# GpSimd subtracts the first expert block's first five weight pieces, and the third block's up weights are requested half by half in another order

## The reference, cut to what matters

```python
def hierarchical_moe(h, w_router_group, w_router_expert, w1, w3, w2):
    xt = h.reshape(T, D); xf = xt.astype(jnp.float32)
    p_group = jax.nn.softmax(xf @ w_router_group, axis=-1)
    g_idx = jnp.argmax(p_group, axis=-1)
    g_w = jnp.take_along_axis(p_group, g_idx[:, None], axis=1)[:, 0]
    local = jnp.einsum('td,gde->tge', xf, w_router_expert)
    local = jnp.take_along_axis(local, g_idx[:, None, None], axis=1)[:, 0]
    top_logit, top_idx = lax.top_k(local, TOP_K)
    gate = jax.nn.softmax(top_logit, axis=-1) * g_w[:, None]
    flat_e = (g_idx[:, None] * EXPERTS_PER_GROUP + top_idx).reshape(-1)
    ...
    def run_block(args):
        xblk, e = args
        hid = jax.nn.silu(xblk @ w1[e]) * (xblk @ w3[e])
        return hid @ w2[e]
    yb = lax.map(run_block, (xb, block_e)).reshape(P, D)
    y = jnp.zeros((T + 1, D)).at[slot_tok].add(yb * slot_w[:, None])[:T]
```

## Time and profile before

| | |
|---|---|
| median of 3 runs | 1733.19 us (1732.63 to 1734.62) |
| profiled execution | 1734.33 us; its span is 1732.5 us |
| granted TensorE clock, mean | 0.979 |
| busy: PE, DVE, ACT, POOL | 1629.7, 1092.2, 861.4, 582.8 us |
| chain that ended last | PE 67%, DMA 15%, DVE 10%, issue 5% |
| DMA | 340.96 MB, mean 197 GB/s; in the experts' stage near 400 GB/s |

### The profile page before, as it was taken

One profiled execution on the slowest core, in us unless ns is written; L12 is line 12 of the kernel. 1 busy time (PEld: TensorE's weight loads), 2 busy tenths in 40 slices (PEclk: granted clock), 3 DMA queues, 4 the chain that ended last, 5 costly groups with the idle time before them and its releaser, 6 DMA issues.

```text
span 1732.5 us, 22014 instructions
## 1 busy us (share of the span) xinstructions
PE 1629.7 (94%) x7052; PEld 1206.6 (70%) x7052; DVE 1092.2 (63%) x1466; ACT 861.4 (50%) x1222; POOL 582.8 (34%) x354
## 2 busy tenths in 40 slices
PE   3899999999999999999999999895999999999996
PEld 3788888777878788778866887583655656656654
DVE  6776865371322458433575543236899999999996
ACT  4544533433222332234443234333878878877875
POOL 0578886333334335324302331110121222222221
PEclk9999999999999999999999999996999999999998
DMA  9343444133131163532211411356999999999993
GB/s 322 104 117 113 136 155 156 59 142 104 49 104 51 47 219 134 194 121 93 98 49 49 152 49 50 89 218 250 375 400 401 395 406 403 393 400 384 384 385 123
DMA packets 135423, 340.96 MB, mean 197 GB/s; under 512 B 14596, under 2 KB 66060, under 8 KB 110521
## 3 DMA queue, kind: packets, MB, share of 16 engines
q1 hardware_dynamic: 127938, 320.71, 49.9%
q0 software_dynamic: 5200, 8.41, 2.1%
q10 hardware_dynamic: 2215, 10.93, 1.6%
HBM read 329.78 MB, written 18.87 MB: 201 GB/s over the span
## 4 chain that ended last, share of the span: by engine, by line
PE 67%; DMA 15%; DVE 10%; issue 5%; ACT 2%; DVEq 0%; SPq 0%; POOLq 0%; ACTq 0%; POOL 0%
PE ps L767 17%; PE ps L769 17%; PE ps L768 17%; DMA ring<-in_w 13%; PE ps L739 6%; DVE parts L2335 3%; PE ps L981 2%; PE ps L749 2%; PE ps L1111 2%; DVE act_parts L2335 1%; DVE arena L2378 1%; PE ps L950 1%; PE ps L1009 1%; PE ps L1092 1%; DMA ring<-in_w_ada 1%
## 5 line engine op out<-in xcount | busy, mean ns | idle before, releaser
L2451 POOL TENSOR_TENSOR parts<-ring,parts 128x1024 fp32r<-128x1024 f32 x156 | 385.6, 2477 | 670.8 <-ACT parts L1209 571.9
L1209 ACT CAST parts<-ring 128x1024 fp32r<-128x1024 f32 x158 | 164.0, 1048 | 347.3 <-PE ps L769 312.1
L767 PE MATMUL ps<-parts,act_parts 128*128 128x512 f32 (+2 forms) x768 | 299.5, 390 | 4.2 <-DVEq L1864 3.0
L769 PE MATMUL ps<-parts,act_parts 128*128 128x512 f32 (+2 forms) x768 | 296.0, 385 | 0.0
L768 PE MATMUL ps<-parts,act_parts 128*128 128x512 f32 (+2 forms) x768 | 296.0, 385 | 0.0
L767 PE MATMUL ps<-act_parts,parts 128*128 128x512 f32 x640 | 252.0, 394 | 4.9 <-DVEq L1769 4.9
L768 PE MATMUL ps<-act_parts,parts 128*128 128x512 f32 x640 | 249.7, 390 | 0.0
L769 PE MATMUL ps<-act_parts,parts 128*128 128x512 f32 x640 | 249.6, 390 | 0.0
L1556 ACT CAST parts<-ring 128x1024 fp32r<-128x1024 f32 x144 | 144.4, 1047 | 83.7 <-PE ps L769 79.1
L767 PEld LDWEIGHTS ps<-parts,act_parts 128*128 128x128 f32 (+1 forms) x768 | 137.4, 179 | 64.8 <-issue 28.1
L2335 DVE TENSOR_TENSOR parts<-ring,parts 128x1024 fp32r<-128x1024 f32 x144 | 168.9, 1218 | 7.4 <-ACT parts L1556 7.2
(11 more groups left out here) (294 smaller groups left out, 2561.8 us busy)
## 6 DMA issues: line engine op xcount, KB each, us to landing
arena<-in_w SPq DMA_DIRECT2D x96, 1024.0 KB, 12.2
ring<-in_w SPq DMA_DIRECT2D x96, 1024.0 KB, 13.3
ring<-in_w_in SPq DMA_DIRECT2D x30, 1024.0 KB, 7.3
ring<-in_w_in SPq DMA_DIRECT2D x34, 512.0 KB, 5.1
ring<-in_w_ada SPq DMA_DIRECT2D x12, 1024.0 KB, 10.4
ring<-in_w_ret_out SPq DMA_DIRECT2D x8, 1024.0 KB, 6.3
ring<-in_w_out SPq DMA_DIRECT2D x8, 1024.0 KB, 7.4
ring<-in_w_in SPq DMA_DIRECT2D x16, 256.0 KB, 4.1
```

The source lines that it names most:

```text
L767: pe.matmul(o, lhs[1], rhs[0], start=start, stop=False)
L769: return pe.matmul(o, lhs[0], rhs[0], start=False, stop=stop)
L1209: act.copy(parts[:, g % 4, 0, :], ring[:, st.place(j), k * 1024:(k + 1) * 1024]).then_inc(dense_hi, 1)
L2451: pool.tensor_tensor(parts[:, g % 4, 1, :], ring[:, st.place(j), k * 1024:(k + 1) * 1024], parts[:, g % 4, 0, :].bitcast(F32), ALU.subtrac ...
```

## The change

Three edits. GpSimd subtracts pieces 2 to 6 of the first block, in a loop that stands behind its last dense piece and before it waits for the plan; DVE's subtractions of these five are gone, and it keeps piece 7. ACT casts piece 6 behind piece 5, before its two Exp. SP requests the third block's up weights in the order w1's second half, w3's first, w1's first, w3's second, with `planned(2)` read once; waits and places of each half are the same as before.

```diff
-            def expert_weights(j, expert, odd, landed=None, used=None):
+            def expert_weights(j, expert, odd, landed=None, used=None, halves=(0, 1)):
...
-                for n in range(2):
+                for n in halves:
...
-            up_weights(planned(2), 0, 32, 1)
+            third = planned(2)
+            for j, half in ((0, 1), (1, 0), (0, 0), (1, 1)):
+                expert_weights(j, third, 0, 32, 1, halves=(half,))
             up_weights(planned(3), 1, 48, 2)
-            expert_weights(2, planned(2), 0, 32, 1)
+            expert_weights(2, third, 0, 32, 1)
...
-            for n in range(2, 6):
+            for n in range(2, 7):
                 high(n, 0, 0)
...
             high_rows("moe0", 0)
-            high(6, 0, 0)
             high(7, 0, 0, used=(up_used, 1))
...
-            for n in (2, 3, 4, 5):
-                low(n, n - 2, 0)
-
             dve.wait_ge(gate_ready, 2)
...
             rest("moe0", 0, xgT)
-            for n in (6, 7):
-                low(n, n - 2, 0)
+            low(7, 5, 0)
...
             lows(len(PIECE_CHUNK))
 
+            for n in range(2, 7):
+                pool.wait_ge(piece_hi, n - 1)
+                pool.tensor_tensor(piece_parts(n)[:, 1, :], expert_place(n // 4, 0)[:, n % 4 * 1024:(n % 4 + 1) * 1024],
+                                   piece_parts(n)[:, 0, :].bitcast(F32), ALU.subtract).then_inc(piece_split[n], 1)
             pool.wait_ge(h3_stored, 16)
```

## The result

The changed kernel takes **1740.38 us** (median of 6 runs, 1736.85 to 1744.05); the kernel before, run beside it, 1733.05 us (6 runs, 1732.4 to 1734.62). The ratio is 1.0041, with a 95% interval of 1.0031 to 1.0051: slower by 7.3 us. The forecast was 1743.7 us in a range of 1738.5 to 1748.5. The profiled execution took 1740.28 us, with a span of 1738.5.

The account below looks back on a forecast made before the run. The routing stage was taken as bound by the latency of DVE's string, then one gather. Terms 0 + 7.0 + 3.5 = +10.5 us on the profiled 1734.33 gave 1744.8, 1743.7 us for the median; range 1738.5 to 1748.5.

Parts of the forecast that it names:

- rival A: Routing: the forecast itself, hold plus disturbed gather, 1739.6 to 1747.7 us; chance 0.85, of it 0.2 with an undisturbed gather.
- one of its own signs of being wrong: First gather in the routing: the prediction would be wrong if it landed in under 4.5 us.
- What the edits take away: Routing and first block: five subtractions leave DVE, but all that time was hidden, so 0.
- The hold: Routing: GpSimd's five subtractions hold DVE's two-input instructions in its string of small dependent ones; +7.0 us, bounds 6.4 to 10.7.
- two alternatives for L2233: DVE's string in the routing: this two-input instruction (L2232 before) is held by the first or second subtraction, to 1173.9 at latest.
- upper bound of 10.7: DVE's string: the hold costs +10.7 us if MAX8, the search and the reduction are held too.
- The gather: First block's token gather, after the routing: slowed to 6.9 us by weights requested earlier; +3.5 us, bounds 0 and +3.8.
- upper bound of 3.8: First gather: the most the earlier weight requests were expected to add, +3.8 us.
- rival D: Tail behind the routing: the shift isn't handed on whole to the end, 1737 us; chance 0.04.
- B: DVE's string: no hold on short instructions, which slip in between; 1736.7 us, or 1733.2 with an undisturbed gather; chance 0.08.
- C: Behind 1191 us: something PE waits for comes earlier, so the kernel is faster, down to 1730.3 us; chance 0.03.
- the same 540.8 us: From the first L1111 to the end: duration expected to stay 540.8 us, within 1.

Follow-up runs that it names:

- The kernel with two pieces behind the gather: Changed kernel, but GpSimd subtracts only pieces 2 and 3, behind its first gather, VectorE the other three; new request order: 1734.01 us, ratio 0.9999.
- both traces of the changed kernel: The changed kernel's first profile and a second execution of it, unchanged; the second gave 1741.13 us (4 runs), ratio 1.0045.
- GpSimd's part alone: Changed kernel with SP's old order of requests, GpSimd's five subtractions kept: 1739.88 us (6 runs), ratio 1.0037.
- The kernel with two pieces: Changed kernel with GpSimd subtracting only pieces 2 and 3, pieces 4 to 6 back on VectorE behind the plan: 1741.62 us, one run.
- Requests alone: Kernel before with SP's new order of requests only, VectorE subtracting as before: 1733.78 us (10 runs), ratio 1.0000.
- eighths: Changed kernel with each GpSimd subtraction cut into eight of 128 columns: 1740.02 us, one run.
- memset kernel: Changed kernel with three GpSimd memsets in place of each subtraction: 1740.63 us in one run, then 1736.77 us (12 runs), ratio 1.0015.
- before again: The kernel before, unchanged, executed once more for a second profile: 1734.11 us, one run.
- two pieces with the old order: Changed kernel with GpSimd subtracting only pieces 2 and 3, and SP's old order of requests: 1736.73 us (11 runs), ratio 1.0018.
- five behind it: Changed kernel with the same five GpSimd subtractions moved behind the issue of the first gather: 1741.16 us (5 runs), ratio 1.0041.
- the unused matmuls: Kernel before with 27 matmuls that nothing reads added on PE in the routing: 1739.66 us (12 runs), ratio 1.0027.

## Why the prediction was right

**Direction and size.** Slower, in the range, 3.3 us below the forecast. The prediction named the case inside its rival A in which the gather gets through ahead of the weights' packets, at 1740 to 1741 us, and gave it 0.2 of 0.85. This is what happened, 1740.38, except that the gather was not quite undisturbed. The forecast itself took the other case, and one of its own signs of being wrong came true: the gather landed in 3.71 us, under 4.5. The sum is off by 3.3 us and not by more partly by luck, since a term that it lacked, below, makes up for some of what it gave the gather too much.

**What the edits take away: 0.** PE's waits name no subtraction before or after, and ACT's Exp still waits for DVE, for 8.52 us. The kernel with two pieces behind the gather, two fifths of that work dealt out where no one waits, is level with before: right.

**The hold: +7.0 forecast, +6.7 measured** in both traces of the changed kernel and in the one with GpSimd's part alone. The instructions that are held in the string, the end of each hold with a subtraction's end and the free DVE behind the fifth came as described. Of its two alternatives for L2233, the first or the second subtraction, the trace has the second. L2248 was held less than foretold, 0.5 us and not 1.5 to 2.5. The form was described too narrowly: two inputs from SBUF are held, but so are a cast and a TENSOR_SCALAR with one. The trace of before had such a row already, beside those that the prediction chose: L1764, TENSOR_SCALAR from SBUF to SBUF with one tensor beside its columns, takes 546 ns at the median and 2364 under a subtraction. It changed nothing here, because the one cast in the stretch began as the first subtraction ended. The upper bound of 10.7 (searches held as well) is excluded by the rows. The kernel with two pieces has one hold of 2.1 us: the term goes by the number of subtractions that meet an instruction they hold, and not by their share (two fifths of 6.7 would be 2.7).

**The gather: +3.5 forecast, +0.3 measured.** This is the mis-sized term. Against GpSimd's part alone, in which the gather has no weights beside it, it is +0.7. The rows it was taken from (5.0 and 7.2 us) are gathers issued into weights that were already flowing; the first gather is issued 0.95 us ahead of the first request. The prediction saw the case and weighed it low. What it did not see is a second cause in it: the subtractions that leave VectorE also free GpSimd's issue of the gather (1.56 to 1.12 us), which brings its first packet from 2.2 to 1.8 us behind the issue, ahead of the weights' 2.1. With VectorE's subtractions still there, in the kernel with two pieces, the term is 7.45 - 3.40 = 4.05 us, a little above the upper bound of 3.8. Requests alone cost nothing for another reason: there they wait for VectorE's subtractions, and the first goes out at 1187.43, 1.95 us behind the gather.

**The two rules of the Trainium skill.** By the rule of ports in the Trainium skill (SBUF — State Buffer, Who interferes with whom) the prediction put the hold at 6.4 to 7.1; the trace agrees with 6.7, and TENSOR_REDUCE kept its 0.38 us. But the prediction gave that rule without its exception. The Trainium skill says there that a DVE instruction with at most one SBUF input is free of GpSimd only outside the two-port modes (one instruction takes both of VectorE's ports), that casts and `tensor_scalar` can enter such a mode, and that one with two SBUF inputs contends only with a GpSimd instruction that reads SBUF. The rows agree with each part: casts and TENSOR_SCALAR held under memsets (0.40 to 0.95 us) and under subtractions (0.32, 0.38, 2.23), two-input rows held under subtractions alone. The other rule of the Trainium skill (DMA: Bandwidth & Descriptors, Issuing engines are not separate DMA queues) says only that the transfers interleave; read as an even share, the prediction's estimate by it was 0.7 for the gather. The measured +0.7 looks like it, but the mechanism is not an even share: with two pieces the gather's packets stood behind 1.02 MB of weights, and in eighths the same lead went with 1.8 us instead of 0.7.

**What the sum lacked.** The clock of PE in the first block. The changed kernel's two L1111 take 11.5 us together, before's 10.0 to 10.4: +1.1 to +1.5 that no term held. It is not tied to the length of the string alone, since GpSimd's part alone shows 10.2, and the memset kernel, with a string only 1.5 us longer than before's, 11.2 and 11.5. The granted clock shows what the sum is made of: in before again and with GpSimd's part alone it came back late, 5.5 and 5.9 us into the block, stayed up, and the second L1111 took 3.65 us; in the twelve other traces it came back sooner, fell to 0.50 once more around the second L1111, and that one took 5.24 us or more. Why a kernel gets the one or the other was not settled.

**The sum again.** 6.7 + 0.3 + 1.1 = 8.1 us up to the third L1111 (8.6 with the second trace of before), and 7.3 us (5.4 to 8.8) in the medians. The shift is handed on: the kernels' shifts to the third L1111 of 6.1, 2.7, 2.5, 0.2, 6.3 and 8.1 us (GpSimd alone, two pieces with the old order, memsets, two behind the gather, five behind it, changed) go with 6.4, 3.1, 2.6, 0, 7.1 and 7.1 us in the ratios, whose intervals reach 1.5 to 2.4 us to either side. So rival D, in which much of the shift is lost on the way, falls, as B does with the held rows and C with the sign. The prediction's own test, the same 540.8 us from the first L1111 to the end within 1, was missed, with 544.8: 1.1 by the clock, 2.9 by the tail, which differs by 2.5 between the two executions of the changed kernel. The test was finer than a single trace allows.

## What to carry to other kernels

Before an idle GpSimd is given work, look at what VectorE does in the same microseconds, not at whether GpSimd is free: a string of short, dependent instructions waits for the end of the GpSimd instruction under way at each instruction of a form that it holds. Here these were instructions with two inputs from SBUF, casts and TENSOR_SCALAR; the price, 2.1 us for two subtractions and 6.7 for five, could be told from eight rows of another stage. Before you write down which forms are free, look for every form of the string under such an instruction, not only for those at hand. The same work is free where both engines have slack, but then look at what is queued behind it on GpSimd: five subtractions ahead of a second gather cost as much as the hold. Of two transfers issued within a microsecond, which one's packets come first made most of the difference here, so give a price for either order.

## What the runs showed that I had not expected

- GpSimd memsets, which read nothing, hold fewer VectorE forms than its subtractions do: casts and TENSOR_SCALAR on small tiles went from 0.17 to between 0.40 and 0.95 us, two-input instructions stayed at 0.17 and 0.29. The string grew by 1.5 us. Subtractions hold both kinds, but neither MAX8 nor the reduction.
- The hold goes the other way as well: GpSimd's issue of an indirect gather took 1.12 us alone and 1.56 us beside VectorE's two-input subtraction, and two of its subtractions 5.64 instead of 4.66 us.
- Beside GpSimd's part alone (3.14 us to the transposes), a gather whose packets come 0.35 us ahead of the weights' lost 0.6 to 0.7 us in four traces and 1.8 in the one with eighths; one whose packets would have come about as much behind them started its packets 5.1 us behind its issue.
- PE came back to 2.4 GHz between 2.9 and 5.9 us into the first block, in kernels that hardly differ there (the one with the unused matmuls left out), and the sum of its first two L1111 varied between 10.0 and 11.5 us.
